# Three edits of one program: first-group steps of a scan stage reordered, head sums of keys moved to the vector engine, embedding products moved into the last head pair

## The reference, cut to what matters

```python
h = h + mamba2_mixer(h, ...)                  # 4 groups of channels, chunked scan
h = per_layer_embedding(h, p[0], ...)
k = rmsnorm_2(kv[..., :SB_WIDTH].reshape(bsz, s, 16, 64), k_g)    # by head
h = h + stick_breaking_mixer(h, k, v, ...)
h = per_layer_embedding(h, p[1], ...)

def per_layer_embedding(h, p_i, norm_g, w_gate, w_proj):
    return h + (p_i @ w_proj) * jax.nn.sigmoid(rmsnorm_2(h, norm_g) @ w_gate)
```

## Time and profile before

| | us |
|---|---|
| three runs, median (lowest, highest) | 3284.34 (3283.60, 3288.83) |
| profiled execution, its own time | 3283.73 |
| profiled execution, span from first to last instruction | 3282.3 |

### The profile page before, as it was taken

One profiled execution on the slowest core, in us unless ns is written; L12 is line 12 of the kernel. 1 busy time (PEld: TensorE's weight loads), 2 busy tenths in 40 slices (PEclk: granted clock), 3 DMA queues, 4 the chain that ended last, 5 costly groups with the idle time before them and its releaser, 6 DMA issues. The chain is left out here.

```text
span 3282.3 us, 40235 instructions
## 1 busy us (share of the span) xinstructions
PE 3098.2 (94%) x15516; PEld 2584.3 (79%) x15516; DVE 1825.8 (56%) x2488; ACT 1387.3 (42%) x2094; POOL 682.7 (21%) x455
## 2 busy tenths in 40 slices
PE   6999998999999999998999999998899999997798
PEld 5788887888888877776787878776688888886677
DVE  4244222666676533255757566575457777776343
ACT  4333221555555423334244252434246666666231
POOL 3110001222223100302001020100234444443110
PEclk8999999999999999999999999999899999998899
DMA  2111212112111234112121121211211111111321
GB/s 93 41 51 49 71 64 71 59 55 68 58 52 65 84 110 145 44 34 71 39 71 52 46 81 41 77 46 58 79 45 40 39 39 39 39 41 43 122 77 52
DMA packets 55861, 201.14 MB, mean 61 GB/s; under 512 B 6544, under 2 KB 9616, under 8 KB 55440
## 3 DMA queue, kind: packets, MB, share of 16 engines
q1 hardware_dynamic: 46288, 166.36, 15.0%
q0 software_dynamic: 9408, 32.51, 3.2%
HBM read 167.26 MB, written 23.20 MB: 58 GB/s over the span
## 5 line engine op out<-in xcount | busy, mean ns | idle before, releaser
L114 ACT ACTIVATE whi<-wraw 128x1024 fp32r<-128x1024 f32 x208 | 218.4, 1050 | 445.9 <-PE a_D L127 59.4
L119 DVE TENSOR_TENSOR wlo<-wraw,whi 128x1024 fp32r<-128x1024 f32 x173 | 232.5, 1344 | 154.3 <-ACT whi L114 153.2
L125 PE MATMUL ssm_D<-x1hi,whi 128*128 128x512 f32 x640 | 259.7, 406 | 14.6 <-issue 9.8
L125 PE MATMUL b_D<-x1hi,whi 128*128 128x512 f32 x640 | 255.2, 399 | 8.5 <-DVEq L1006 6.6
L127 PE MATMUL ssm_D<-x1hi,wlo 128*128 128x512 f32 x640 | 251.9, 394 | 0.0
L126 PE MATMUL ssm_D<-x1lo,whi 128*128 128x512 f32 x640 | 251.9, 394 | 0.0
L126 PE MATMUL b_D<-x1lo,whi 128*128 128x512 f32 x640 | 250.8, 392 | 0.0
L127 PE MATMUL b_D<-x1hi,wlo 128*128 128x512 f32 x640 | 250.8, 392 | 0.0
L2365 DVE TENSOR_TENSOR_SCAN stick_keep<-stick_keep 128x896 f32<-128x896 f32 (+7 forms) x128 | 215.1, 1681 | 43.8 <-ACT stick_keep L2273 42.5
L2504 POOL TENSOR_TENSOR stick_rows<-stick_rows,stick_keep 128x896 f32<-128x896 f32 (+7 forms) x128 | 162.8, 1274 | 271.8 <-DVE stick_keep L2365 271.5
L125 PE MATMUL stick_D<-x1hi,whi 128*128 128x512 f32 x512 | 210.4, 411 | 6.8 <-DVE x1lo L152 6.8
(11 more groups left out here) (443 smaller groups left out, 7942.1 us busy)
## 6 DMA issues: line engine op xcount, KB each, us to landing
wraw<-w_dram SPq DMA_DIRECT2D x208, 512.0 KB, 3.5
sq<-acum_rows SPq DMA_DIRECT2D x32, 512.0 KB, 3.8
att_bias<-alibi_dram SPq DMA_DIRECT2D x16, 512.0 KB, 3.6
stack<-stack POOLq DMA_DIRECT2D x32, 256.0 KB, 3.7
x_sb<-xT_dram SPq DMA_DIRECT2D x8, 512.0 KB, 9.6
branch_a<-sq POOLq DMA_DIRECT2D x8, 512.0 KB, 3.5
y_b<-att_y POOLq DMA_DIRECT2D x8, 512.0 KB, 3.0
f<-y_b SPq DMA_DIRECT2D x2, 2048.0 KB, 8.8
```

Source lines behind the costliest of these rows:

```text
L114: act.activation(self.whi[:, s, :, :], self.wraw[:, s, :, :], ACT.Copy).then_inc(self.w_hi, 1)
L119: dve.tensor_tensor(self.wlo[:, s, :, :], self.wraw[:, s, :, :], self.whi[:, s, :, :].bitcast(F32), ALU.subtract).then_inc(self.w_lo, 1)
L125: pe.matmul(out, self.whi[:, s, w0, :], xhi[:, k, cols], start=start, stop=False)
```

## The change

It has three parts.

1. In ssm, group 0: the spread of the first norm stands after 12 units instead of 16; the two additions of squares are on DVE instead of POOL; and the extra DVE steps, which stood behind the weight split of a tile, now stand behind the scaling of single halves (`opening`), one final-norm operation after each half of tiles 2 to 5.
2. In stick: the keys are transposed first (slots 6 and 7). ACT squares the transposed half out of PSUM and copies it to SBUF (`copy_k`), DVE adds the squares by head over the whole tile (`sum_k`, slot 7), ACT takes the root (slot 8), DVE scales the whole tile in SBUF (`norm_k`, slot 8). The PE sums for the keys are gone; those for the queries stay.
3. The embedding product of ple1 is computed in the last pair of stick: 16 half-tiles of six matrix instructions (`embed_half`) by the table `EMBED_HALVES`, after the score row of slots 4 to 18, into `stick_D`. Their factors are loaded and split into the `x1hi` memory in slots 2 to 4; ACT copies each half-tile to SBUF (`embed_copy`), SP stores them to DRAM (`embed`), and ple1 loads the eight tiles back and multiplies from SBUF. Its own loads, splits and products of that kind are gone.

```diff
-                units(g, 0, KT, 2 * KT)
+                units(g, 0, KT, KT + 4)
                 pe.wait_ge(rt_step, 5)
                 spread_factor(rt)
+                units(g, 0, KT + 4, 2 * KT)
...
+            for i, acc in enumerate((K.acc, K.R)):
+                dve.wait_ge(sq_base, i + 1)
+                dve.tensor_tensor(acc[:, :], acc[:, :], K.sq[:, i, :], ALU.add).then_inc(acc_base, 1)
...
+        def opening(c, half):
+            if half == 0 and c == 1:
+                step_sizes()
+            if half == 0 and c == 3:
+                decay_sums()
+            if half == 0 and c == 4:
+                decay_ends()
+            if c >= 2:
+                final_norm(2 * (c - 2) + half)
...
                     scale(g, 2 * c + half, u[:, c % 2, :], half)
+                    if g == 0:
+                        opening(c, half)
...
+EMBED_HALVES = {4: (0,), 5: (1,), 6: (2,), 7: (3,), 8: (4,), 9: (5,), 10: (6,), 11: (7,), 12: (8,), 13: (9,),
+        14: (10,), 15: (11,), 16: (12,), 17: (13,), 18: (14, 15)}
+AUX_SLOT = dict(k_turn0=6, k_turn1=7, k_sum=8, k_back0=9, k_back1=10, v_turn0=12,
...
+        sp.dma_start(e_raw[0], io["pT"][1].rearrange("(k p) t -> p k t", p=P)).then_inc(e_land, 16)
+        sp.dma_start(e_raw[1].rearrange("p a (b m) -> p (a b) m", m=P).rearrange("p (j k) m -> p j k m", k=2),
+                     io["w_ple"][1].rearrange("j p k m -> p j k m")).then_inc(e_land, 16)
+        sp.wait_ge(e_low, 2)
...
+        for j in range(KT):
+            sp.wait_ge(e_copy, 2 * j + 2)
+            sp.dma_start(embed[j, :, :], K.sq[:, j % 2, :]).then_inc(e_left[j % 2], 16)
...
-            if g == 0:
-                pe.wait_ge(rooted, 2 * p + 1)
+            if g == 1:
+                pe.wait_ge(k_copied, 2 * p + 1)
             else:
-                pe.wait_ge(kn_done, 2 * p + 1)
+                pe.wait_ge(evac, 8 * p + (2 * TK + 4))
+                if p > 0:
+                    pe.wait_ge(rooted, 2 * p)
...
+        def embed_half(n):
+            j, half = n // 2, n % 2
+            if n == 0:
+                pe.wait_ge(e_low, 2)
+                pe.wait_ge(evac, 8 * PAIRS + 2)
+            elif n >= 2:
+                pe.wait_ge(e_copy, n - 1)
+            cols = slice(half * H, half * H + H)
+            for k in range(2):
+                pe.matmul(D[:, cols], e_w[0][:, j, k, :], e_hi[0][:, k, cols], start=k == 0, stop=False)
+                pe.matmul(D[:, cols], e_w[0][:, j, k, :], e_lo[0][:, k, cols], start=False, stop=False)
+                last = pe.matmul(D[:, cols], e_w[1][:, j, k, :], e_hi[0][:, k, cols],
+                                 start=False, stop=k == 1)
+            last.then_inc(e_mm, 1)
...
+                if not more:
+                    for n in EMBED_HALVES.get(slot, ()):
+                        embed_half(n)
...
+        def copy_k(p, g):
+            cols = slice(g * H, g * H + H)
+            act.wait_ge(k_turn, 2 * p + (g + 1))
+            if g == 0 and p > 0:
+                act.wait_ge(summed, p)
+            act.activation(square[:, cols], pV[:, :], ACT.Square)
+            act.activation(kN[:, cols], pV[:, :], ACT.Copy).then_inc(k_copied, 1)
...
+        def embed_copy(n):
+            j, half = n // 2, n % 2
+            cols = slice(half * H, half * H + H)
+            act.wait_ge(e_mm, n + 1)
+            if n >= 4:
+                act.wait_ge(e_left[j % 2], 16 * (j // 2))
+            act.activation(K.sq[:, j % 2, cols], D[:, cols], ACT.Copy).then_inc(e_copy, 1)
...
+                    if slot in (2, 3):
+                        act.wait_ge(e_land, 32)
+                        act.wait_ge(dn, 8 * PAIRS)
+                        act.activation(e_hi[slot - 2], e_raw[slot - 2], ACT.Copy).then_inc(e_high, 1)
+                    for n in EMBED_HALVES.get(slot - 1, ()):
+                        embed_copy(n)
...
+        def sum_k(p):
+            dve.wait_ge(k_copied, 2 * p + 2)
+            dve.reduce_sum(k_sum[:, :], square.rearrange("p (a d) -> p a d", d=HD), axis=mybir.AxisListType.X).then_inc(k_summed, 1)
+        def norm_k(p):
+            by_head = kN.rearrange("p (a d) -> p a d", d=HD)
+            dve.tensor_tensor(by_head, by_head, k_inv[:, :].unsqueeze(2).to_broadcast([P, 16, HD]),
+                              ALU.mult).then_inc(kn_done, 2)
...
+            if slot == AUX_SLOT["k_turn1"]:
+                sum_k(p)
             if slot == AUX_SLOT["k_sum"]:
                 inverse_k(p)
+                norm_k(p)
...
+                if not more and slot in (3, 4):
+                    dve.wait_ge(e_high, slot - 2)
+                    dve.tensor_tensor(e_lo[slot - 3], e_raw[slot - 3], e_hi[slot - 3].bitcast(F32),
+                                      ALU.subtract).then_inc(e_low, 1)
...
+        else:
+            for j in range(KT):
+                sp.dma_start(unused[:, j, :], embed[j, :, :]).then_inc(e_land[j], 16)
...
+                if embed is None:
+                    dve.wait_ge(pm, n + 1)
+                    product = pP[:, s, :]
+                else:
+                    dve.wait_ge(e_land[n], 16)
+                    product = unused[:, n, :]```

The order of DVE in group 0 of ssm, tiles 3 and 4, before. `wlo` is the weight split, `heads_*` are `decay_ends`, `f` is the final norm, `sq<-ssm_D,R` the scaling of a half, `ssm_xs` a tap:

```order
L119 TENSOR_TENSOR wlo<-wraw,whi 128x1024
L1765 TENSOR_TENSOR heads_dte<-heads_dte,heads_dt 128x256
L1766 TENSOR_SCALAR heads_acum<-heads_acum 128x256
L1772 SCALAR_TENSOR_TENSOR f<-f,vec,ssm_pY 128x1024 x2
L1711 TENSOR_TENSOR sq<-ssm_D,R 128x512 x2
L1831 SCALAR_TENSOR_TENSOR ssm_xs<-sq,vec,ssm_xs 128x1021
```

More of the change, by code:

```diff
@@ L2017, in stage_stick @@
         y_left, y_free, dma_go = sem("y_left"), sem("y_free"), sem("dma_go")
+        e_land, e_high, e_low, e_mm, e_copy = sem("e_land"), sem("e_high"), sem("e_low"), sem("e_mm"), sem("e_copy")
+        e_left = [sem("e_left0"), sem("e_left1")]
+        e_raw = [f_sb[:, 2 * i:2 * i + 2, :] for i in range(2)]
+        e_hi, e_lo = ([x[:, 2 * i:2 * i + 2, :] for i in range(2)] for x in (xhi[:, 0:4, :], xhi[:, 4:8, :]))
+        e_w = [t[1].rearrange("p a (b m) -> p (a b) m", m=P).rearrange("p (j k) m -> p j k m", k=2) for t in (e_hi, e_lo)]
         with nc.Block() as block:
@@ L2324, in pair @@
                             ahead(p + 1, 1 - q, slot)
+                    if not more:
+                        for n in EMBED_HALVES[18]:
+                            embed_copy(n)
                     part_y(p, 7)
@@ L2428, in aux @@
                             low_v(p, q, g)
-                        if slot == AUX_SLOT[f"k_turn{g}"]:
-                            norm_k(p, g)
                     if slot == AUX_SLOT["q_sum"]:
@@ L2645, in _ @@
                     K.dense(pe, D[:, s, :], s, xhi, xlo, x_lo if j == 0 else None).then_inc(mm, 1)
+                    if embed is not None:
+                        if j == 0:
+                            K.norm_spread(pe, spread, rtok_done, 1, spread_done)
+                        continue
                     if j == 0:
@@ L2661, in _ @@
                     last.then_inc(pm, 1)
-                    if j == 0 and squared:
-                        K.norm_spread(pe, spread, rtok_done, 1, spread_done)
             @block.scalar
```

120 lines of the change are left out of this document (56 added, 64 removed).

## The result

The changed kernel takes 3261.87 us (median of 4 runs, 3258.35 to 3262.11) beside 3284.63 for the kernel before on the same chip: a ratio of 0.9926, 95% interval 0.9909 to 0.9943, so 24 us faster by the ratio and between 19 and 30. The profiled execution took 3258.35 with a span of 3256.8, 25.5 under the span of before (3282.3); it was the fastest of the four, the others took 3261.76 to 3262.11.

The account below looks back on a forecast made before the run. PE's own work was taken to bound regular pairs of stick, the chain between engines the last pair. Parts of -15, +7.5 and -7.8 us summed to -15.3, giving 3269 us from the median, range 3248 to 3284.

Parts of the forecast that it names:

- rival B: Last pair of stick: factors come earlier or holes take more, +4 instead of +12.7 us, total 3261; chance 0.13.
- the first hole and its clock: First group of ssm: four units cover PE's 2.2 us wait at the spread, and 1.7 us of lower clock goes.
- the long wait: First group of ssm: PE's 9.8 us wait for the eighth final norm ends 7.6 us earlier, leaving about 2 us.
- the clock behind it: At ssm's z tiles: lower clock after the shortened wait partly remains, so half of 2.4 us is gained, -1.2.
- masks of the first chunk: First group of ssm: z begins before tile 5's taps are done, so these may come late, +0.5 us.
- some 7: First group of ssm: DVE's scaling, norm, taps and split per tile in us, covered by a tile of 10.9 us.
- rival E: Regular pairs: everything added in slots 7 to 9 lies on the path, +4.7 us a pair, total 3298; chance 0.07.
- rival A: Regular pairs: keys' scaling gets through before POOL or `values` has more cover, saving all 13.7 us, total 3248; chance 0.12.
- my 13.7 covered: Last pair: of 21.8 us of added PE work, waits in 15 slots cover 13.7 and leave 8.1 us.
- -3 for that: Last pair: PE's work at low clock returns to full clock, giving back 3 us.
- low clock in and behind slot 4: Last pair: after a 4.7 us stall the half-tile runs at lower clock (2.4 us), and some following work too (1.4).
- The ple1 term: In ple1: embedding products no longer stand before or between the gate tiles, -20.5 us.

Follow-up runs that it names:

- part 1 alone: Kernel before with only the first group of ssm changed: 3270.36 us, ratio 0.9951.
- no_root: Changed kernel with the root of the keys' mean squares replaced by a plain copy, so no table load for it: a regular pair takes 81.17 us.
- pool_waits: Changed kernel with POOL's multiplication of row 8 made to wait until DVE has scaled the keys: a regular pair takes 80.98 us.
- parts 1 or 2 alone: Kernel before with only the first group of ssm changed (3270.36 us), or only the keys of the second attention (3292.02 us, ratio 1.0020).
- PE's edit alone: Kernel before with only PE's spread of the norm moved four units earlier: 3286.57 us, one execution.
- part 3 alone: Kernel before with only the embedding product moved into the last pair: 3270.01 us, ratio 0.9962.

## Why the prediction came out

**Direction and size.** Forecast 3269 (3248 to 3284), measured 3261.9: inside the range, 7 us faster than the point (by the ratio, -24 us against -15.3). It lies next to rival B's 3261, and half of B came: the last pair cost less, but through the clock, not through earlier factors or more holes. By parts, in the profile's ledger:

| part | forecast | trace | alone, by ratio |
|---|---|---|---|
| 1 | -15 | -17.0 | -16 |
| 2 | +7.5 | +5.3 | +7 |
| 3 | -7.8 | -14.3 | -12 |

**Part 1** came by its own steps: the first hole and its clock 3.9 forecast, 4.0 seen; the second 2.6 and 2.7; the long wait 7.6 and 7.8, with 2.1 us left where I said about 2. For the clock behind it I took half of 2.4, since a wait of 2.2 us had brought 0.70 at 1414. In this trace and in part 1 alone the remaining wait of 2.13 us brought none, and all 2.4 were gained. That is luck of the execution: the other eight kernels have the same first group and the same wait of 2.13 us, and behind it the clock was 0.64 to 0.66 over 4.8 us. The window of no_root at that place:

```profile
1471.27:1476.07 4.80, 4.80 (x14) 3.83 (x15) 4.69 (x4) 1.75 (x2) 0.00 (x0) 0.66 0.00 0
```

The first twelve z products took 4.3 to 4.4 us in those eight, 2.8 here and 5.3 before, so 0.9 us was gained there, near the 1.2 of the forecast, and part 1 is nearer to -15.5 than to -17 in most executions. The 0.5 for the masks of the first chunk didn't show: with part 1 alone the lead is still 17 us at the second group's spread. And "some 7" us for scaling, norms, taps and split of a tile was too little; DVE's rows add up to 9.0 (1.4, 2.5, 3.9 and 1.2), still under the 10.9 of PE's tile.

**Part 2** has the right sign, and its place and mechanism stood as forecast: scaling 2.47 us, ended 1.1 behind POOL, values waiting 1.56 (forecast about 2), a pair at 81.17 (81). Behind slot 9 PE came to row 10 0.71 us later than before (forecast 0.7), to row 11 0.92 and to the next pair 0.94 (I took 1.2), and ahead of the first pair 1.3 us were saved instead of 0.9: so +5.3 and not +7.5. Its upper end, +20, has no working: rival E's own sum is 32. What the working lacked is that the wait for the split is one of three of nearly one length. I followed the split and row 9's product, gave the table loads a delay of 0.6 us, and did not ask what would be late if the split were early. The experiments did: row 9's sigmoids, then its running product and POOL's product of it. So my rival A had its condition wrong: the scaling getting through before POOL (pool_waits) does not save the 13.7 us, it saves 0.2 a pair.

**Part 3** holds the larger error, and it is one term. Window of the kernel before, from row 0 to the last values:

```profile
2984.84:3049.68 64.84, 39.95 (x212) 33.69 (x212) 43.54 (x45) 37.83 (x62) 24.61 (x19) 0.79 0.02 9
```

and its PE waits in the changed kernel, same frame:

```profile
PE stick_scores L2135 <- ACT stick_rows L2323: 6.1, 2, 3.8
PE stick_turned L2153 <- POOL stick_rows L2580: 4.9, 4, 2.7
PE stick_D L2195 <- DVE x1hi L2533: 4.8, 1, 4.8
```

Waits fell from 24.8 to 15.8 us, by 9.0: my 13.7 covered less 4.7 in slot 4 are 9.0 as well. But PE's own time rose from 40.0 to 56.6, by 16.6 instead of 21.8: with the holes filled the mean clock went from 0.79 to 0.88 and the old work ran faster. I had -3 for that, and against it low clock in and behind slot 4 (2.4 in place of the 0.9 left of that half-tile, and 1.4), -0.1 together; it was -5.2. This is the term that was mis-sized. So the pair cost 7.5 us, not 12.7. How much of this belongs to the change is less sharp than one trace looks: with the same last pair as before, the three kernels with parts 1 or 2 alone, or with PE's edit alone, took 66.6 to 66.9 us for it instead of 64.84, at another pattern of clocks (0.76 to 0.77). And with the half-tiles of the changed kernel and the same last pair it took 72.3 to 73.4 us in six traces, at 0.86 to 0.88. Against those three the half-tiles cost 5.4 to 6.8 us. What decides which pattern comes stays open. The ple1 term was 20.5 forecast and 21.4 to 21.8 seen.

In the stall of slot 4 there is something I left out: POOL's product of row 4, which started 0.22 us behind DVE's split of 2048 columns, took 3.22 us, against 1.32 for a row of the same 640 columns at 2831.91 in a regular pair of the same trace.

## What to carry to other kernels

Before counting time that an engine saves inside a repeated stretch, ask for each of its next few waits how much slack the other engine has there: here 1.35 us on PE ended on three chains of nearly one length that hid each other, so that taking away one gave 0.17 or nothing. Work that is to fill an engine's holes is best spread at one piece a hole, put where its operands are long ready, and its remainder belongs in the wait between two stages; and where the holes had lowered the clock, filling them pays a second time. An operation of DVE with two SBUF inputs is put in the plan by its neighbour on POOL: 1.22 us alone, 2.47 beside one that had started first, and what has to be planned is its end (here 1.08 us behind POOL's end), not its start. And a term of the clock wants more than one trace: the same wait in the same code brought 1.00 in two and 0.65 in eight.

## What the runs showed of the hardware

- The same short wait of PE was not always followed by the same clock. Behind the 2.13 us ahead of the z tiles it was 1.00 over 4.8 us in two traces (changed kernel, part 1 alone) and 0.64 to 0.66 in eight, with the same code before it and PE at full clock until then. Behind 2.57 us ahead of tile 4 it was 1.00 over 5 us in the kernel before (1466.2) and 0.66 with part 3 alone (1463.84), again in the same code. Behind 9.8 us it was 0.50 to 0.51 over 4.8 us in all four kernels that have this wait.
- The reduction by head, which no row of before showed, takes 1.22 us for 1024 columns to 16 values, as much as an elementwise operation of that size; POOL was idle beside it, so what it takes beside POOL wasn't seen.
- The contention goes both ways, and each time the one that started second paid. DVE's split of 2048 columns kept its 2.26 us in the last pair, while POOL's products that started 0.22 us behind it took 2.53 us for 256 columns (0.64 in a regular pair) and 3.22 for 640 (1.32). In slots 8 and 9 POOL started first and kept its 1.78 us, and DVE's scaling took 1.89 to 2.75 instead of 1.22.
- The sigmoid followed the table load at once here too (2851.14 + 1.28 = 2852.42, sigmoid at 2852.43).
